# Expert slots of 32 rows on four column quarters, with the gate and up weights laid side by side by copies during the first mixers

## The reference

```python
expert = (g_idx * EXPERTS_PER_GROUP + e_idx).reshape(-1)     # 2048 x 2 choices
order = jnp.argsort(expert)
xs = tok[order // TOP_K]
sizes = jnp.bincount(expert, length=N_EXPERTS)
hg = lax.ragged_dot(xs, w_gate, sizes)                       # 1024 -> 256 each
hu = lax.ragged_dot(xs, w_up, sizes)
ys = lax.ragged_dot(jax.nn.silu(hg) * hu, w_down, sizes)     # 256 -> 1024
out = jnp.einsum('nkd,nk->nd', ys[inv].reshape(N, TOP_K, D), weights)
```

## Time and profile before

| | |
|---|---|
| Median of 3 runs | 4731.66 us (4728.71 to 4732.94) |
| The profiled execution's own time | 4731.05 us |
| Its span, first to last instruction | 4729.2 us |
| PE busy | 4326.1 us, 91% |
| DVE, ACT, POOL busy | 53%, 29%, 16% |
| Mean granted TensorE clock | 0.95 |
| Bytes moved by DMA | 714.58 MB, mean 151 GB/s |

### The profile page before, as it was taken

The page is one execution under the profiler, slowest core; times in us unless marked ns, Lnnn a source line. Parts: engine busy times, 40 slices in busy tenths (PEclk is TensorE's granted clock), DMA queues, the critical chain, the costliest instruction groups (busy, mean ns, idle before and its releaser), DMA issues. The chain is left out here.

```text
span 4729.2 us, 62656 instructions
## 1 busy us (share of the span) xinstructions
PE 4326.1 (91%) x22613; PEld 2638.9 (56%) x22613; DVE 2494.7 (53%) x5856; ACT 1385.0 (29%) x2851; POOL 770.1 (16%) x767
## 2 busy tenths in 40 slices
PE   7799999999968999979799999999948889989998
PEld 6466666666633333335365454545437768777775
DVE  4543434343442232336478999999946555542222
ACT  1133333333310111113267110100136667650000
POOL 0001010101014555532131000000011121000001
PEclk9799999999978999989899999999969989999999
DMA  9655555555507676756564444444553142123221
GB/s 295 218 185 150 187 148 190 145 192 143 187 29 282 228 270 239 265 204 208 156 167 127 125 114 133 115 117 114 161 150 86 50 103 70 46 97 112 89 89 62
DMA packets 688757, 714.58 MB, mean 151 GB/s; under 512 B 195464, under 2 KB 539744, under 8 KB 674400
## 3 DMA queue, kind: packets, MB, share of 16 engines
q1 hardware_dynamic: 594352, 498.10, 35.3%
q0 software_dynamic: 63024, 191.60, 11.7%
q10 hardware_dynamic: 31104, 21.24, 1.4%
HBM read 770.69 MB, written 135.09 MB: 192 GB/s over the span
## 5 line engine op out<-in xcount | busy, mean ns | idle before, releaser
L1937 PE MATMUL l_unit<-l_xT,l_w 128*128 128x512 f32 x2048 | 909.7, 594 | 29.0 <-DMA l_xT<-mid_xn3T 29.0
L1937 PEld LDWEIGHTS l_unit<-l_xT,l_w 128*128 128x128 f32 x2048 | 387.5, 190 | 465.6 <-issue 457.6
L2035 DVE TENSOR_SCALAR_CACHE_REDUCE l_work<-l_score,l_trial 128x384 bf16<-128x384 f32 (+1 forms) x434 | 617.2, 1475 | 8.9
L417 PE MATMUL f_ring<-f_win,f_hT 128*128 128x512 f32 x1024 | 464.0, 609 | 14.3 <-issue 8.5
L1319 PE MATMUL e_ph<-e_gateup,e_rowsT 128*64 128x512 f32 x1536 | 343.7, 600 | 5.2 <-DVE e_rowsT L1479 5.2
L417 PEld LDWEIGHTS f_ring<-f_win,f_hT 128*128 128x128 f32 x1024 | 195.3, 195 | 254.6 <-issue 242.2
L2370 DVE CUSTOM_DVE_ANT_0 sparse_scores<-sparse_s,sparse_pen 128x512 f32<-128x512 f32 (+3 forms) x320 | 182.7, 608 | 159.8 <-PE sparse_s L124 140.0
L2479 PE MATMUL o_branch<-o_y,w_branches 128*128 128x128 f32 x2048 | 233.5, 277 | 13.5 <-DMA o_gates<-mid_gzT 13.5
L2479 PEld LDWEIGHTS o_branch<-o_y,w_branches 128*128 128x128 f32 x2048 | 233.3, 194 | 20.4 <-issue 20.4
L2491 PE MATMUL o_out<-w_last,o_merged 128*128 128x512 f32 x512 | 225.5, 599 | 5.2 <-POOL o_merged L2461 5.2
L525 PE MATMUL f_ring<-f_wout,f_trio 128*128 128x512 f32 x512 | 226.4, 601 | 1.4 <-DVE f_trio L898 1.4
(11 more groups left out here) (384 smaller groups left out, 6940.1 us busy)
## 6 DMA issues: line engine op xcount, KB each, us to landing
f_win<-in_w_in SPq DMA_DIRECT2D x64, 2048.0 KB, 8.1
l_w<-in_w_in SPq DMA_DIRECT2D x144, 512.0 KB, 4.1
f_win<-in_w_in SPq DMA_DIRECT2D x128, 256.0 KB, 5.0
f_wout<-in_w_ada SPq DMA_DIRECT2D x24, 1024.0 KB, 12.0
mid_ys<-e_out SPq DMA_DIRECT2D x48, 512.0 KB, 3.8
f_win<-in_w_in SPq DMA_DIRECT2D x16, 1024.0 KB, 6.9
mid_gzT<-l_out SPq DMA_DIRECT2D x64, 256.0 KB, 4.0
o_gates<-mid_gzT SPq DMA_DIRECT2D x16, 1024.0 KB, 8.3
```

The costliest lines, as they stand in the source:

```text
L417: mm = nc.tensor.matmul(to[:, :], hT[:, k, :], w[:, k, :], start=(k == 0), stop=(k == KD - 1))
L1937: mm = nc.tensor.matmul(pu[n % 2][:, :], w[:, n % WB, k, :], xT[:, t % 2, k, :], start=(k == 0), stop=(k == KD - 1))
L2035: V.tensor_scalar(unread, score(b), at_least(b), None, op, ALU.add, accum_out=count[:, b:b + 1])
```

## The change

A slot has 32 rows instead of 64, and there are 160 instead of 96. Four lanes of two phases replace two lanes of three, so there are 40 steps and eight streams of 20 turns; each lane multiplies on a quarter of TensorE's columns. A new scratch tensor `gate_up` holds each expert's gate and up rows side by side, 16 KB per partition row; POOL fills it during the first mixers with two copies from memory to memory per finished block, and the experts load gate and up with one indirect transfer per lane. The gathered rows have one buffer instead of three, and the results leave by quarters of 256 columns through three small buffers, four stores a step. The order of POOL's loop changes to gather, gate and up, then the down load of the step before. Many small tables of the experts' routing now lie in buffers that are free at that time, the index arithmetic finds stream and lane by comparisons, and the gate row goes through memory to a tile of the combine stage.

```diff
-SLOT, NS = 64, 96
+SLOT, NS = 32, 160
...
 (stage_front, gpsimd)
+                    if s == GATES_AT + 1:
+                        pool.wait_ge(read["gr"], 2)
+                        settle(g, pool)
+                        pool.dma_start(g.gate_row[0:1, :], gate[0:1, 1, :]).then_inc(gate_stored, 16)
                     if t is not None:
                         pool.wait_ge(xn2_ready, t + 1)
                         settle(g, pool)
                         pool.dma_start(g.x1[t * P:(t + 1) * P, :], xb[:, t % 4, :]).then_inc(x1_stored, 16)
                         pool.dma_start(g.xn2[t * P:(t + 1) * P, :], xn2).then_inc(xn2_stored, 16)
+
+                        rows = slice(2 * t * P, (2 * t + 2) * P)
+                        for n, w in enumerate((g.w_exp_gate, g.w_exp_up)):
+                            pool.dma_start(g.gate_up[rows, n * KD * FF:(n + 1) * KD * FF],
+                                           w[0].rearrange("e (p k) f -> (e p) (k f)", p=P)[rows, :]).then_inc(pair_stored, 16)
...
+                pool.wait_ge(gate_stored, 16)
+                pool.wait_ge(pair_stored, 32 * NB)
                 pool.wait_ge(x1_stored, 16 * NB)
...
 (stage_experts)
-    LANES, PHASES = 2, 3
+    LANES, PHASES = 4, 2
...
-    RING = 3
+    RING, QUARTER = 3, D // 4
...
-        xg = sb("e_rows", [P, RING, D])
+        xg = sb("e_rows", [P, D])
...
-                for t in range(STEPS):
-                    sp.wait_ge(y_read, 2 * t + 2)
-                    sp.dma_start(g.ys[t * P:(t + 1) * P, :], ys[:, t % RING, :]).then_inc(stored[t % RING], 16)
+                for n in range(4 * STEPS):
+                    t, c = n // 4, n % 4
+                    sp.wait_ge(y_read, n + 1)
+                    sp.dma_start(g.ys[t * P:(t + 1) * P, c * QUARTER:(c + 1) * QUARTER], ys[:, n % RING, :]).then_inc(stored[n % RING], 16)
...
                     for lane in range(LANES):
-                        for n, w in enumerate((g.w_exp_gate, g.w_exp_up)):
-                            load(w[0].rearrange("e (p k) f -> (e p) (k f)", p=P), wgu[:, stream(t, lane), n, :, :].rearrange("p k f -> p (k f)"), t, lane, gu_loaded)
+                        load(g.gate_up[:, :], wgu[:, stream(t, lane), :, :, :].rearrange("p a k f -> p (a k f)"), t, lane, gu_loaded)
...
-                    if t >= RING:
-                        pool.wait_ge(xT_done, t - RING + 1)
+                    if t:
+                        pool.wait_ge(xT_done, t)
...
                 gather(0)
                 load_up(1)
+                gather(1)
                 load_down(1)
-                gather(1)
-                load_up(2)
-                load_down(2)
-                gather(2)
                 for t in range(PHASES, STEPS):
+                    gather(t)
                     load_up(t)
-                    gather(t)
-                    load_down(t)
+                    if t > PHASES:
+                        load_down(t - 1)
+                load_down(STEPS - 1)
...
 (scalar)
-                        for n in range(2):
-                            act.wait_ge(down_done, 2 * (t - 1) + n + 1)
-                            nc.scalar.activation(ys[:, u, n * 512:(n + 1) * 512], py[:, n, :], ACT.Copy).then_inc(y_read, 1)
+                        for c in range(4):
+                            n = 4 * (t - 1) + c
+                            if n >= RING:
+                                act.wait_ge(stored[n % RING], 16 * (n // RING))
+                            act.wait_ge(down_done, 2 * (t - 1) + c // 2 + 1)
+                            nc.scalar.activation(ys[:, n % RING, :], py[:, c // 2, c % 2 * QUARTER:(c % 2 + 1) * QUARTER], ACT.Copy).then_inc(y_read, 1)
...
 (vector, index arithmetic)
+                for n in range(2, STREAMS):
+                    v.drain()
+                    V.scalar_tensor_tensor(out=at[:, STREAM, :], in0=at[:, IN_ORDER, :], scalar=float(n * TURNS), in1=at[:, STREAM, :], op0=ALU.is_ge, op1=ALU.add)
+                    if n < LANES:
+                        V.scalar_tensor_tensor(out=at[:, LANE, :], in0=at[:, IN_ORDER, :], scalar=float(n * TURNS * PHASES), in1=at[:, LANE, :], op0=ALU.is_ge, op1=ALU.add)
...
 (stage_combine, scalar)
                 act.dma_start(rope[:], g.c_rope.rearrange("(b p) n -> p b n", p=P)).then_inc(rope_loaded, 16)
+                act.dma_start(gate[:], g.gate_row[0:1, :].to_broadcast([P, D])).then_inc(gate_loaded, 16)
```

More of the change, by code:

```diff
@@ L245, in stage_front @@
         vec = sb("f_vec", [P, 88])
+        gate = sb("f_gate_rows", [P, 2, D])
         vec2 = sb("f_vec2", [P, 3, KD])
@@ new lines, in stage_experts @@
+        ac = g.tables[:, 0:FF]
+        ys = g.tables[:, FF:FF + RING * QUARTER].rearrange("p (u n) -> p u n", u=RING)
+        spare = [wgu[:, PHASES * n + 1, :, :, :].rearrange("p a k f -> p (a k f)") for n in range(LANES)]
+        in_row = [spare[n][:, 0:NB * P].rearrange("p (b r) -> p b r", b=NB) for n in range(2)]
+        in_step = spare[2][:, 0:2 * NB * STEPS].rearrange("p (n b r) -> p n b r", n=2, b=NB)
+        tables = spare[3][:, 0:5 * NB * NE].rearrange("p (n b e) -> p n b e", n=5, b=NB)
@@ new lines, in stage_experts @@
+        oh, both, tmp, place = tables[:, 0:2, :, :], tables[:, 2, :, :], tables[:, 3, :, :], tables[:, 4, :, :]
+        room = lambda at_, n: spare[3][:, 5 * NB * NE + at_:5 * NB * NE + at_ + n]
+        ex = room(0, 3 * NS).rearrange("p (a n j) -> p a n j", a=3, n=STREAMS)
+        at = room(3 * NS, 16 * NB).rearrange("p (a n) -> p a n", a=8)
+        past = room(3 * NS + 16 * NB, NS)[0:NE, :]
+        over = room(4 * NS + 16 * NB, SLOT * 2)[0:NE, :]
+        n_col = room(4 * NS + 16 * NB + 2 * SLOT, 2)[0:NE, :]
@@ L1220, in stage_experts @@
         gu_loaded, d_loaded = ([sem(f"{n}_{u}") for u in range(STREAMS)] for n in ("gateup_loaded", "down_loaded"))
-        gathered, stored = ([sem(f"{n}_{u}") for u in range(RING)] for n in ("gathered", "stored"))
+        gathered = sem("gathered")
+        stored = [sem(f"stored_{u}") for u in range(RING)]
         stream = lambda t, lane: PHASES * lane + t % PHASES
@@ L1286, in _ @@
                 pe.wait_ge(onehots, 1)
-                nc.tensor.matmul(ph[:, 0, :], before, both[:].rearrange("p b e -> p (b e)"), start=True, stop=False)
+                nc.tensor.matmul(ph[:, 0, :], before, both.rearrange("p b e -> p (b e)"), start=True, stop=False)
                 nc.tensor.matmul(ph[:, 0, :], ones, g.counts[:, 0:NB, :].rearrange("p b e -> p (b e)"), start=False, stop=True).then_inc(ranked, 1)
@@ L1312, in up @@
                     for lane in range(LANES):
-                        pe.wait_ge(gu_loaded[stream(t, lane)], 32 * (t // PHASES + 1))
+                        pe.wait_ge(gu_loaded[stream(t, lane)], 16 * (t // PHASES + 1))
                     pe.wait_ge(xT_read, t + 1)
@@ L1318, in up @@
                         for lane in range(LANES):
-                            mm = nc.tensor.matmul(ph[lane_cols(lane), t % 2, :], xT[:, k, lane_cols(lane)], wgu[:, stream(t, lane), :, k, :],
+                            mm = nc.tensor.matmul(ph[lane_cols(lane), t % 2, :], xT(k)[:, lane_cols(lane)], wgu[:, stream(t, lane), :, k, :],
                                                   start=(k == 0), stop=(k == KD - 1), tile_position=(0, lane * SLOT))
@@ L1357, in _ @@
                 act.wait_ge(group_arg, 1)
-                nc.scalar.activation(gt[:], gt[:], ACT.Exp).then_inc(group_exp, 1)
+                nc.scalar.activation(gt, gt, ACT.Exp).then_inc(group_exp, 1)
                 act.wait_ge(pair_arg, 1)
@@ L1514, in stage_combine @@
         ng = sb("b_gain", [P, KD])
+        gate = sb("b_gate", [P, D])
         to_rows = sb("b_to_rows", [P, 2, NB], U32)
```

149 lines of the change are left out of this document (69 added, 80 removed).

## The result

| | before | after |
|---|---|---|
| Median (9 runs each) | 4731.18 us (4724.87 to 4735.18) | 4742.97 us (4739.45 to 4750.74) |
| Ratio, 95% interval | | 1.003 (1.0021 to 1.0038) |
| Span of the profiled execution | 4729.2 us | 4739.7 us |
| Mean granted TensorE clock | 0.95 | 0.94 |

The change made the kernel slower by 0.3%. The forecast was 4681 us with a chance of 0.8 for faster: wrong in size and in sign. 4742.97 lies 1 us above the top of the range.

The account below looks back on a forecast made before the run. TensorE was taken to bound the mixers and experts as long as no transfer is late. Experts -103.5, copies +46, seams +4.5 and +3 summed to -50 us, from 4731.05 to 4681 us, range 4634 to 4742.

Parts of the forecast that it names:

- A quiet step stays at 12.06 us: Experts: four column quarters run at once, so the step is unchanged; 37 periods in place of 45, -96.5 us.
- The last rival: Experts: quarters don't overlap fully at 512 columns; 30% longer products give 4810 us; chance 4%.
- Part 2, the bursts: Experts' transfers: two changed lanes just fit, three come 5 us late; stalls 18 in place of 29.0, -11 us.
- Part 3, the late g4 loads: Mixers: copies delay SP's load for project(p, 4), called g4, by 2.15 us on the mean in 14 blocks, +46 us.
- g5: Mixers: the load behind g4's on SP's queue lands at 753.3, needed at 754.6, so in time.
- The factor of 1.53: Mixers and experts: a microsecond of waiting costs 29.0/19.0 = 1.53 us, as in the experts' stretch before.
- Part 4, the seams: Mixers' end and combine stage: last copies delay the experts' start, +4.5 us; the gate row's broadcast adds +3 us.
- The gate row: Head of the combine stage: its 0.5 MB broadcast goes ahead of the gains the vector engine waits for, +3 us.
- the start: Experts' first steps: first loads are 12.6 MB in place of 6.3, so turn_rows(2) starts later, +3 us.
- The rival of bursts: Experts bound by issue or bursts, costing 20 to 35 us, 4700 to 4716; chance 13%.
- each double 3 us late: Experts, within the rival of bursts: every step with two changed lanes 3 us late, costing 20 to 35 us.
- The rival of late loads alone: Mixers: slower through g4's loads alone, from 4.5 us of lateness a block; 5.95 would give 4762 us; chance 13%.

Follow-up runs that it names:

- before_plus_copies: Kernel before with the 32 memory-to-memory copies added to POOL's stream, nothing reading what they write: 4808.72 us, ratio 1.0161.
- copies_sp: Kernel after with the copies issued by SP on its own queue, behind the load the mixers need next: 4773.5 us, ratio 1.0089.
- no_loads: Kernel after with the expert loads of steps 2 to 39 left out: 4683.11 us.
- after_again: Kernel after with nothing altered, a control on another chip: 4846.05 us, ratio 1.0246.
- up_loads_only: Kernel after with the down loads left out after the first two steps, so four indirect loads a step instead of eight: 4747.98 us.
- skip_unchanged: Kernel after with POOL branching past the indirect load of a lane whose expert stays, a 64-byte copy in its place: 4757.91 us, ratio 1.0041.
- copies_2k: Kernel after with each 8 KB copy row written as four columns; packets stayed at 8 KB, so in effect unchanged: 4848.6 us, ratio 1.0252.
- copies_2k_rows: skip_unchanged with the copies' columns outermost so pieces can't be joined; packets became 4 KB: 4877.83 us, ratio 1.0306.

## Why the prediction was wrong

Two steps failed by size: the lateness of the expert loads (40 us) and that of the g4 loads (16 us). A third, 6 us, left out a term.

- **A quiet step stays at 12.06 us.** Right where the time was measured: 12.03 in after, 64 up instructions in 7.0 us. 32 full-width instructions of 512 columns take 14.00 us, so four quarters run four times as fast at 512 columns too. On three other chips most steps took 15.7 to 16.7 us, and the whole 4846 to 4858 us. The last rival had that outcome (4810 us, 4%), but for another reason: the quarters do overlap fully, up to the ninth group.
- **Part 2, the bursts: this step failed most, 40 us.** It had 18 us of stalls; after has 504.0 - 37 x 12.03 = 59. The two steps of three lanes were forecast at 15 us of it, the seven doubles at 3 together. But each of the doubles was late, and the six that stand by themselves cost 5.4 to 7.9 us each. The text counted two changed lanes as 10 us of bytes and 4 more, which "just fit" in 16.2. Measured at step 12: the rows are turned at 1680.5, POOL starts the gather at 1681.3, the weights' packets move from 1685.7 to about 1698.7, and the up block starts at 1699.87. So 5.2 us pass ahead of the bytes, 13.0 with them and 1.2 behind them, 19.4 instead of 14. The 4.19 MB ran at 0.32 MB/us and not at the 0.42 of the earlier trace rows. SP's stores had 9.4% of the engines from 1686 to 1699, which is under half of the difference; the packets of skipped loads and of the next gather had another 10%. This double is 3.29 us late and costs 6.1: the wait, and 8.14 us for products of 5.36 at a granted clock of 0.50 in the first 4 us.
- **Part 3, the late g4 loads: right in kind, 16 us too small.** g4 landed 21.2 us behind its issue where the sum had 20.3, and over the 14 blocks PE waited 3.0 us on the mean (2.0 to 5.4) where it was put at 2.15. g5 landed in time, as said. before_plus_copies shows that the copies alone cost it, copies_sp that behind SP's loads they cost next to nothing (the last weight product at 1311.3 instead of 1307.4). The mechanism rests on the trace: in each of the eleven microseconds from 431 to 442 the two queues' packet counts differ by four at most, at some 2 of each per engine. With turns of many packets, an engine would move only one queue's through most of such a microsecond, and over 16 engines the counts would scatter more than that (an estimate from these counts; no run changed the turns). That the packet size sets the delay, no run showed.
- **The factor of 1.53 held.** The blocks lost 61.9 us for 42.3 of waiting, 1.46, and the experts 59 for 39.6, 1.49. What failed in both parts is how late the loads are.
- **Part 4, the seams: a term was left out.** The last copy landed 17.7 us behind the last store's issue, where the sum had 17.5. But then POOL's drain took 5.38 us ahead of the barrier, and the experts began 7.0 us behind the landing instead of 1.4: +10.9 instead of +4.5. In the kernel before, the same drain took 2.69 us and was over long before DVE reached the barrier. With SP's copies (copies_sp) the seam is 13.7 us, as before. Why the drain takes longer behind POOL's copies no run shows. The gate row cost 3.7 instead of 3, the start 5.1 instead of 3. All had the right sign.
- **The rival of bursts** (13%, 4700 to 4716) was the nearest to what happened in the experts, though it put its extra at 20 to 35 us; "each double 3 us late" was right for the one at step 12. The rival of late loads alone (slower, 13%) asked for 4.5 us of lateness a block and got 3.0. The forecast held the two apart, and both came about together. Both errors have one sign: transfers were slower beside each other than the rows from quieter stretches said (0.32 MB/us instead of 0.42, g4 landing in 21.2 us instead of 20.3).
- **Not foreseen at all:** the long steps. What is shown: they need the expert loads as POOL issues them (no_loads has 12.03 us, its control 16.7); they come with half the bytes (16.1), and two steps of after_again in which no weight bytes move at all (15 and 34) take 16.5 us like their neighbours; the four loads left in up_loads_only bring less of them than the eight elsewhere (12.7 us against 15.7 to 16.7); POOL's memsets don't bring them (12.03); PE's results are late ahead of them (DVE's copy 0.43 us behind the up block's start instead of 0.10). Not shown is how the loads delay TensorE, and why the chips of the result don't have them. The kernel before issues seven such transfers a step and takes 571.7 and 570.1 us in the two traces kept, one of them on a chip with long steps; whether its two column halves spare it, or its lower rate of instructions, wasn't tried.

## What to carry to other kernels

Try a background copy on the queue that carries the urgent loads, behind them, before one on a queue of its own beside them: here the same 67 MB cost some 70 us more one way than the other. For a burst of loads, count the time from release to need with the rate that the queue has beside its neighbours in that very stretch, and add the slower clock after the wait (0.32 MB/us and not 0.42, and a granted clock of 0.50 for 4 us, at step 12). Look at what an engine still does between a landing and a barrier (here a drain of 5.38 us). An indirect transfer whose rows are all skipped is not free (0.99 us of POOL and 128 packets here): try a branch past it, and time a kernel with dense GpSimd transfers on more than one chip before trusting a gain.

## What the runs showed of the hardware

- An indirect load with every row out of bounds still takes POOL 0.99 us and leaves 128 packets of 4 bytes; with 244 of them gone (skip_unchanged) the software queue had 47888 packets instead of 75216. A register load, a branch and a 64-byte copy took about 0.9 us together, 0.5 of it the copy.
- The same program ran its expert step in 12.03 us where the result was measured and mostly in 15.7 to 16.7 us on three other chips, at a granted clock of 1.00, while the kernel before took the same time everywhere within 0.1%.
- Contiguous pieces of a copy were joined to 8 KB packets (copies_2k); pieces that can't be joined made the copy slower as a whole (copies_2k_rows), with 1.69 us of issue for 0.57 and 36.5 us to the second one's landing for 18.7 in after.
- POOL's drain ahead of the barrier took 5.3 to 5.4 us behind its own copies, 2.7 to 2.8 us without them, and 0.32 us behind the unjoined copies of copies_2k_rows.
